# A running sum on GpSimd in place of eight products with ones in the trunk norms of a two-layer diffusion backbone (one core)

## The reference: what is computed

```python
def rms_norm(x, g):
    xf = x.astype(jnp.float32)
    y = xf * lax.rsqrt(jnp.mean(xf * xf, axis=-1, keepdims=True) + EPS)
    return (y * g.astype(jnp.float32)).astype(x.dtype)

def ffn_sublayer(t, shift, scale, gate, g_pre, g_post, w_in, w_out):
    y = swiglu(modulate(rms_norm(t, g_pre), shift, scale), w_in, w_out)
    return t + FFN_RES * gate * rms_norm(y, g_post)
```

## Time and profile before

| | |
|---|---|
| Median of three runs | 3211.84 us (3211.83 to 3213.26) |
| Span of the profiled execution, first to last instruction | 3222.9 us |
| Mean granted TensorE clock | 0.944 |
| PE busy | 2937.8 us (91%) |
| DVE busy | 1645.7 us (51%) |
| ACT busy | 1185.0 us (37%) |
| POOL busy | 253.7 us (8%) |

### The profile page before, as it was taken

One profiled execution on the slowest core, in us unless ns is written; L12 is line 12 of the kernel. 1 busy time (PEld: TensorE's weight loads), 2 busy tenths in 40 slices (PEclk: granted clock), 3 DMA queues, 4 the chain that ended last, 5 costly groups with the idle time before them and its releaser, 6 DMA issues.

```text
span 3222.9 us, 40926 instructions
## 1 busy us (share of the span) xinstructions
PE 2937.8 (91%) x14458; PEld 2316.6 (72%) x14458; DVE 1645.7 (51%) x2616; ACT 1185.0 (37%) x2119; POOL 253.7 (8%) x319
## 2 busy tenths in 40 slices
PE   6999979768998989997999979999797899899897
PEld 5888858546855865675888858888584877759897
DVE  4776254663345333434566256762545445435754
ACT  3222232353245233434222342222434434344543
POOL 0000011120000000001000010000111100000101
PEclk8999989888989998998999989999899989999899
DMA  5555313302300221021455315553230321223554
GB/s 224 170 196 178 97 51 111 98 1 65 92 26 1 89 65 46 27 91 65 138 176 178 96 64 181 193 176 91 67 108 20 117 67 47 90 64 125 182 176 137
DMA packets 93530, 337.13 MB, mean 105 GB/s; under 512 B 10866, under 2 KB 12658, under 8 KB 91506
## 3 DMA queue, kind: packets, MB, share of 16 engines
q1 hardware_dynamic: 74274, 263.45, 25.4%
q0 software_dynamic: 19152, 72.36, 7.1%
HBM read 334.71 MB, written 1.06 MB: 104 GB/s over the span
## 4 chain that ended last, share of the span: by engine, by line
PE 76%; issue 8%; DVE 8%; ACT 5%; POOL 2%; DMA 1%; SPq 0%; DVEq 0%; POOLq 0%; ACTq 0%
PE ps L1405 19%; PE ps L1398 19%; PE ps L1399 19%; PE ps L620 3%; PE ps L658 3%; PE ps L636 2%; PE ps L1432 1%; DVE mx L537 1%; PE ps L1429 1%; PE ps L1434 1%; PE ps L616 1%; ACT work L897 1%; PE ps L615 1%; DVE work L1151 1%; ACT prob L483 1%
## 5 line engine op out<-in xcount | busy, mean ns | idle before, releaser
L1058 DVE TENSOR_TENSOR wlo<-raw,whi 128x1024 fp32r<-128x1024 f32 x488 | 592.0, 1223 | 679.8 <-ACT whi L842 679.3
L1398 PE MATMUL ps<-xhi,whi 128*128 128x512 f32 (+1 forms) x2304 | 823.6, 368 | 53.3 <-DVE xlo L1184 44.9
L1399 PE MATMUL ps<-xlo,whi 128*128 128x512 f32 (+1 forms) x2304 | 814.5, 364 | 0.0
L842 ACT ACTIVATE whi<-raw 128x1024 fp32r<-128x1024 f32 x488 | 516.4, 1059 | 753.6 <-PE ps L1405 680.6
L1398 PEld LDWEIGHTS ps<-xhi,whi 128*128 128x128 f32 x2304 | 443.9, 193 | 142.5 <-issue 41.3
L1405 PE MATMUL ps<-xhi,wlo 128*128 128x512 f32 (+1 forms) x2304 | 504.8, 362 | 0.6 <-DVE wlo L1058 0.6
L1399 PEld LDWEIGHTS ps<-xlo,whi 128*128 128x128 f32 x2304 | 445.4, 193 | 64.1 <-issue 0.5
L1405 PEld LDWEIGHTS ps<-xhi,wlo 128*128 128x128 f32 x2304 | 399.4, 192 | 66.2 <-DVE wlo L1058 1.0
L1100 DVE SCALAR_TENSOR_TENSOR work<-ada,work 128x1024 f32<-128x1024 f32 x256 | 299.4, 1220 | 6.2 <-DMA work<-silu_rows 3.7
L1398 PE MATMUL ps<-ghi,whi 128*128 128x512 f32 (+1 forms) x704 | 252.3, 368 | 1.9 <-ACT whi L842 1.9
L1399 PE MATMUL ps<-glo,whi 128*128 128x512 f32 (+1 forms) x704 | 251.6, 366 | 0.0
(11 more groups left out here) (146 smaller groups left out, 3339.6 us busy)
## 6 DMA issues: line engine op xcount, KB each, us to landing
raw<-in_ffn_in SPq DMA_DIRECT2D x176, 512.0 KB, 4.8
ada<-in_ada_rows POOLq DMA_DIRECT2D x128, 512.0 KB, 3.8
raw<-in_merge SPq DMA_DIRECT2D x96, 512.0 KB, 3.5
raw<-in_ffn_out SPq DMA_DIRECT2D x64, 512.0 KB, 3.6
raw<-in_qk_a SPq DMA_DIRECT2D x32, 512.0 KB, 3.5
raw<-in_ffn_out SPq DMA_DIRECT2D x32, 384.0 KB, 3.1
raw<-in_qk_b SPq DMA_DIRECT2D x20, 512.0 KB, 3.5
raw<-in_v_a SPq DMA_DIRECT2D x16, 512.0 KB, 3.5
```

Source lines behind the costliest of these rows:

```text
L842: act.activation(whi[:, g.ring(SPLIT), :], raw[:, g.ring(RAW), :], ACT.Copy).then_inc(hi_ready, 1)
L1058: dve.tensor_tensor(wlo[:, g.ring(SPLIT), :], raw[:, g.ring(RAW), :], whi[:, g.ring(SPLIT), :].bitcast(F32), ALU.subtract).then_inc(lo_rea ...
L1398: pe.matmul(o, w, hi[:, first + c, 0:tk], start=start, stop=False)
L1399: pe.matmul(o, w, lo[:, first + c, 0:tk], start=False, stop=False)
```

## The change

In a norm with `pre`, POOL adds up the eight squared chunks in `acc`: the first is a copy, the other seven are additions (`running_sum`). Each waits for ACT's square and, by `xsum`, for its own predecessor. ACT squares chunk c when POOL has finished chunk c - 2. PE makes a single product of ones by `acc` when the eighth is in, and signals it by a new semaphore `xstat`, for which ACT's Ln waits. On POOL the additions to x of chunks 1, 3 and 5 stand ahead of the sum of the chunk before each. The memset of `acc` at the start of each phase `y` waits for `xstat` too.

```diff
         if pre:
-            adds.update(xsq=KC, xsum=KC, scaled=KC, shifted=KC, xhi=KC, xlo=KC)
+            adds.update(xsq=KC, xsum=KC, xstat=1, scaled=KC, shifted=KC, xhi=KC, xlo=KC)
...
+            def running_sum(ph, c):
+
+                pool.wait_ge(done["xsq"], base(ph, "xsq") + c + 1)
+                if c == 0:
+                    if ph.post:
+                        pool.wait_ge(done["stat"], base(ph, "stat") + 1)
+                    pool.tensor_copy(acc[:, 0:ph.tokens], tmp[:, 0, 0:ph.tokens]).then_inc(done["xsum"], 1)
+                else:
+                    pool.wait_ge(done["xsum"], base(ph, "xsum") + c)
+                    pool.tensor_tensor(acc[:, 0:ph.tokens], acc[:, 0:ph.tokens], tmp[:, c % 2, 0:ph.tokens],
+                                       ALU.add).then_inc(done["xsum"], 1)
...
-                if ph.kind == "norm" and ph.post:
-                    for n, c in enumerate(POOL_CHUNKS):
-
-                        pool.wait_ge(done["gated"], base(ph, "gated") + c + 1)
-                        pool.tensor_tensor(x[:, c, 0:ph.tokens], x[:, c, 0:ph.tokens], work[:, c, 0:ph.tokens],
-                                           ALU.add).then_inc(done["xp"], 1)
+                if ph.kind == "norm":
+                    for c in range(KC):
+                        if ph.post and c in POOL_CHUNKS:
+
+                            pool.wait_ge(done["gated"], base(ph, "gated") + c + 1)
+                            pool.tensor_tensor(x[:, c, 0:ph.tokens], x[:, c, 0:ph.tokens], work[:, c, 0:ph.tokens],
+                                               ALU.add).then_inc(done["xp"], 1)
+                        if ph.pre and c:
+                            running_sum(ph, c - 1)
+                    if ph.pre:
+                        running_sum(ph, KC - 1)
                 if ph.kind == "y":
 
                     pool.wait_ge(done["stat"], base(ph, "stat"))
+                    pool.wait_ge(done["xstat"], base(ph, "xstat"))
...
-                        inverse(inv[:, 0:tk], STAT, tk, D, base(ph, "xsum") + KC, "xsum")
+                        inverse(inv[:, 0:tk], STAT, tk, D, base(ph, "xstat") + 1, "xstat")
...
                         wait(pe, done["refined"], base(ph, "inv") + (1 if ph.post else 0))
-                        for c in range(KC):
-
-                            pe.wait_ge(done["xsq"], base(ph, "xsq") + c + 1)
-                            pe.matmul(ps[:, STAT, 0:ph.tokens], ones[:, :], tmp[:, c % 2, 0:ph.tokens],
-                                      start=c == 0, stop=c == KC - 1).then_inc(done["xsum"], 1)
+                        pe.wait_ge(done["xsum"], base(ph, "xsum") + KC)
+                        pe.matmul(ps[:, STAT, 0:ph.tokens], ones[:, :], acc[:, 0:ph.tokens], start=True, stop=True)\
+                          .then_inc(done["xstat"], 1)
```

More of the change, by code:

```diff
@@ L303, in build @@
         done = {name: sem(f"{name}_done") for name in (
-            "ghi", "glo", "gated", "xp", "xsq", "xsum", "sq", "acc", "stat", "inv", "x", "scaled", "shifted", "xhi", "xlo", "rope", "m", "mhi",
+            "ghi", "glo", "gated", "xp", "xsq", "xsum", "xstat", "sq", "acc", "stat", "inv", "x", "scaled", "shifted", "xhi", "xlo", "rope", "m", "mhi",
             "mlo", "lsq", "lt", "lhi", "llo", "score", "bias", "exp", "prob", "turned", "pt", "pv",
```

## The result

The changed kernel takes 3255.05 us, the median of four runs (3246.24 to 3257.68), against 3212.55 for the kernel before in the same session. The ratio is 1.011, with a 95% interval of 1.0081 to 1.0139: it is slower. Predicted were 3246 and a range of 3230 to 3257.

What follows compares the result with a forecast made beforehand. The prediction took each norm to be bound by the wait chain through DVE, not by PE; 4 x 7.9 + 3.4 - 1.0 = 34.0 us, added to the median, gave 3246, with a range of 3230 to 3257.

Steps and rivals of the forecast that it cites:

- The bound: In a norm, the wait chain runs through DVE, squares and Ln; removing PE's products removes only the 2.06 us tail.
- The step of 1.68: In 512-token norms, DVE and POOL alternate one instruction each, 1.68 us per pair with an addition.
- The copy's price: POOL's added copy in each norm, not in the trace, was taken as 0.7 us, between 0.54 and 1.27.
- The product with ones: PE's single product replacing the tail before Ln in each norm: 1.12 us from a resting PE.
- The sum: All norms together: 4 x 7.9 + 3.4 - 1.0 = 34.0 us longer, added to the median of the runs.
- Elsewhere nothing: Outside the changed norms no time changes; a shifted clock rise was allowed 2 us in all, either sign.
- (a): Rival: added POOL instructions and DVE don't interfere in the norms; +11 us, 3223; chance 10%.
- (b): Rival: DVE goes first in the norms and POOL's eleven instructions pile up behind; +46 us, 3257; chance 15%.
- (c): Rival: not slower, POOL's sum hidden under DVE in five norms, first norm 5.4 us shorter; 3206; chance 4%.
- the first norm's gain: First norm: ACT no longer waits for PE's shift products; 1.0 us earlier forecast, 5.4 without interference.
- (d): Rival: PE's rest delays the clock's rise after five norms by some 3 us; 7.5 on top, 3253; chance 9%.

Runs made afterwards that it cites:

- The kernel with late sums: The changed kernel, with GpSimd beginning the running sum only after VectorE's last addition to x; 3265.8 us, ratio 1.0141 to the kernel before.
- the one with copies: The changed kernel, with the running sum's seven additions replaced by copies of the squared chunk, so the sum is left out; 3231.08 us, ratio 1.0041.
- the kernel with idle products: The changed kernel, with four unused products on TensorE ahead of each of eight sums in the five later norms; 3253.71 us, ratio 1.0105.

## Why the prediction was right

**The bound.** That a norm is not PE's, and that removing seven of eight products removes only a tail, held: PE's busy time fell by 41 us and the time rose.

**The collision.** The step of 1.68 read from the earlier trace rows is 1.66 to 1.68 in the norms after. The kernel with late sums, the one with copies and the two without POOL's additions to x all came out within 0.5 us per norm of what this one rule gives, but for one 512-token norm of the kernel before without them, which is 0.9 off because PE's slow products bound it. The Trainium skill's "SBUF — State Buffer", section "Who interferes with whom", calls the contention for the shared port pair an exclusive lock; 1.09 beside a copy of 0.61 and 1.74 to 1.76 beside an addition of 1.27 agree.

**The copy's price.** I took 0.7 between 0.54 and 1.27; alone it takes 0.61, beside DVE 1.07.

**The product with ones.** This term of the sum was mis-sized. I wrote 1.12 "from a resting PE", and elsewhere that PE would be at the low clock for this product. But that row's PE had rested 2.03 us behind a busy stretch, and its granted clock was still 1.00, so the two didn't go together. After 23 us of rest the product takes 2.04, which the kernel with idle products brings back to 1.02. It is 0.9 per norm too little. The last sum ended 18.0 behind the first POOL addition where I had 18.5, so of 0.9 only 0.5 is left: 20.25 instead of 19.8 in the second norm. In the third to fifth the order was just the forecast one, the last sum ended 18.3 behind, and it is 20.53: 0.7 too little in each of three.

**A misread row.** I called 449.53 the end of the last square. It is the end of chunk 6's; chunk 7's ends at 450.12, only 1.47 before Ln. The chain goes through chunk 6 because PE's products of both chunks fill the 2 us behind it. The sum doesn't depend on this, since it compares the starts of Ln.

**The sum.** Forecast 4 x 7.9 + 3.4 - 1.0 = 34.0, read from the traces 36.4, of which 33.1 are left in the profiled spans. The medians differ by 42.5 in one session and by 30.4 in the other. That 3255 came out and not 3246 is in the main scatter from run to run: 3211.84, to which I added, lies at the low end of what the kernel before takes (3211.3 to 3228.3).

**Elsewhere nothing.** This step didn't hold. I had written that it would be wrong if the low clock ended at another distance behind the norms. It did behind the third and the fourth, 1.8 and 2.8 us earlier in both profiles of the changed kernel. The other way would have cost time; this way it gave some 2 us back, about what I had allowed for either sign.

**Rivals.** (a), no interference, is refuted by the timeline. (b), DVE first, too: they alternate. (c) had the first norm's gain for it, which is 1.7 at most and not 5.4, because the sum there collides with the dot products: POOL's seven additions take 14.49 us, 2.2 apart where I had 2.4. (d), a later rise of the clock, isn't seen: behind no norm does it rise later than in every profile of the old sum.

## What to carry to other kernels

Take work off the busiest engine only where that engine ends last; in a stage of hand-overs, follow the chain of waits to see whose work that is. Before giving GpSimd a share of elementwise work beside VectorE, look for pairs whose durations grow together: here each 128x512 addition costs VectorE 1.07 us and saves it 0.60, so the helper is a loss even at three per norm, where VectorE is what ends last. And price a product from a row with the same rest ahead of it, not only of the same shape.

## What the runs showed of the hardware that was not expected

- VectorE and GpSimd alternate fairly when both always have two-input work in SBUF: one instruction each, with a period of 1.66 to 1.68 us at 128x512 for a 0.60 and a 1.27 (third norm of the changed kernel). In the second norm POOL's third sum came 0.03 us late, and VectorE got two in a row.
- VectorE's scalar_tensor_tensor with an accumulator is held up as well: 2.16 to 2.17 us instead of 1.23 beside the sum in the first norm, and 1.23 again once it was over.
- A product on 128x512 fp32 took 1.02 us at the full clock and 2.04 after 23 us of rest. With TensorE kept busy through the sum, the products 8 us later were at the low clock all the same (granted 0.50, 0.80 and 0.63 us each).
- In the first norm the same products ran at the low rate until 42.65 in one execution and until 39.50 in another, while the mean granted clock over the stretch from 36.60 to 47.00 reads 1.00 in both. There the instructions' durations tell the rate and that mean doesn't.
- The same kernel's executions differ by up to 17 us (3211.3 to 3228.3) while each 512-token norm between the first and the last repeats to 0.02 us.
